# A 64-byte tile behind the parameter tile: everything allocated after it moves by 64 bytes

## What the kernel computes

```python
# block 1: a gated linear recurrence (stage A, OA), then forgetting attention (FG, F, OF)
x = x + (o * silu(gate)) @ a_w_out             # projections h @ w_in, 4 x 2048 columns
x = x + (attention(q, k, v, F) * silu(gate)) @ b_w_out
# block 2: recurrence and top-k attention side by side (X, C, OC)
x = x + (sigmoid(gr) * y_rnn + sigmoid(ga) * y_attn) @ w_o
# then a layer of 16384 experts, of which each token uses 8 x 16 (stages Q, U, V)
act = gelu(x . u[expert]) * gate               # 16 experts per head and token
x = x + sum(act * v[expert])
out = rmsnorm(x)
```

## The kernel before, in words

| tile | before | with the new tile |
|---|---|---|
| `xT`, `hh`, `hl` | 0 | 0 |
| `raw`, `wl`, `wh`, `iota`, `prm` | 64 | 64 |
| `ident`, `ones` (the pace), `ones_r`, `rstd`, `oT`, `sq`, `act`, `act_odd` | 64 | 0 |
| `kh`, `kl`, `uh_a`, `uh_c`, `ul_c`, `uh_q`, `ul_q`, `ckv_h`, `ckv_l` | 64 | 0 |
| `ah`, `al`, `gates_b`, `hot_a`, `kT_f`, `keysT`, `qp` | 64 | 0 |
| `uk_h`, `uk_l`, `uv_h`, `uv_l`, `xc`, `kT_c`, `qT_c`, `v_c`, `probT_c` | 0 | 64 |
| `AT`, `v_a`, `osq_a` | 32 | 96 |

## Time and profile before

### The profile page before, as it was taken

The page is one execution under the profiler, slowest core; times in us unless marked ns, Lnnn a source line. Parts: engine busy times, 40 slices in busy tenths (PEclk is TensorE's granted clock), DMA queues, the critical chain, the costliest instruction groups (busy, mean ns, idle before and its releaser), DMA issues.

```text
span 3275.2 us, 69109 instructions
## 1 busy us (share of the span) xinstructions
PE 3243.6 (99%) x28331; PEld 3211.1 (98%) x28331; DVE 2260.1 (69%) x3785; ACT 1685.3 (51%) x2279; POOL 33.8 (1%) x46
## 2 busy tenths in 40 slices
PE   9999999999999999999999999999999999999998
PEld 8999999999999999999999999999999999999998
DVE  8767667655566776666678987755676557788755
ACT  5444454767775556565554344444444444444444
POOL 4000000000000000000000000000000000000000
PEclk9999999999999999999999999999999999999999
DMA  5444445444445554545455555555555555555553
GB/s 189 153 148 166 144 162 182 155 155 165 159 162 183 194 171 164 189 164 188 167 188 174 187 181 181 182 185 184 181 180 182 183 186 184 180 175 173 180 182 140
DMA packets 98974, 569.29 MB, mean 174 GB/s; under 512 B 9440, under 2 KB 30304, under 8 KB 31584
## 3 DMA queue, kind: packets, MB, share of 16 engines
q1 hardware_dynamic: 98496, 565.49, 50.8%
q10 hardware_dynamic: 288, 1.05, 0.1%
HBM read 564.41 MB, written 2.10 MB: 173 GB/s over the span
## 4 chain that ended last, share of the span: by engine, by line
PE 90%; DVE 7%; DVEq 1%; ACT 1%; issue 1%; DMA 1%; POOL 0%; POOLq 0%; ACTq 0%; SPq 0%
PE bank L581 20%; PE bank L582 20%; PE bank L583 20%; PE bank L1069 8%; PE bank L1070 7%; PE bank L1071 7%; DVE wl L1652 2%; PE bank L1027 1%; PE bank L735 1%; PE bank L938 0%; PE bank L813 0%; PE bank L812 0%; PE bank L684 0%; DMA raw<-w_out_b 0%; PE bank L970 0%
## 5 line engine op out<-in xcount | busy, mean ns | idle before, releaser
L582 PE MATMUL bank<-hl,wh 128*128 128x256 f32 x5616 | 1563.5, 278 | 0.0
L1652 DVE TENSOR_TENSOR wl<-raw,wh 128x1024 fp32r<-128x1024 f32 x1052 | 1260.5, 1228 | 433.0 <-ACT wh L1151 425.7
L581 PE MATMUL bank<-hh,wh 128*128 128x256 f32 x5488 | 1546.3, 282 | 2.9 <-DVE wl L1652 2.5
L583 PE MATMUL bank<-hh,wl 128*128 128x256 f32 x5488 | 1525.8, 278 | 0.0
L1151 ACT ACTIVATE wh<-raw 128x1024 fp32r<-128x1024 f32 x1052 | 1051.3, 1049 | 270.4 <-DMA raw<-w_in_a 123.4
L582 PEld LDWEIGHTS bank<-hl,wh 128*128 128x128 f32 x5616 | 1060.1, 189 | 1.9 <-issue 1.7
L581 PEld LDWEIGHTS bank<-hh,wh 128*128 128x128 f32 x5488 | 1036.2, 189 | 7.3 <-issue 2.0
L583 PEld LDWEIGHTS bank<-hh,wl 128*128 128x128 f32 x5488 | 1033.7, 188 | 0.0
L1069 PE MATMUL bank<-ah,wh 128*128 128x256 f32 x2048 | 583.2, 285 | 1.4 <-DVE al L2360 1.4
L1071 PE MATMUL bank<-ah,wl 128*128 128x256 f32 x2048 | 580.2, 283 | 0.0
L1070 PE MATMUL bank<-al,wh 128*128 128x256 f32 x2048 | 580.2, 283 | 0.0
(11 more groups left out here) (412 smaller groups left out, 3178.2 us busy)
## 6 DMA issues: line engine op xcount, KB each, us to landing
raw<-peer_u SPq DMA_DIRECT2D x128, 1024.0 KB, 4.9
raw<-peer_v SPq DMA_DIRECT2D x128, 1024.0 KB, 4.8
raw<-w_in_c SPq DMA_DIRECT2D x64, 1024.0 KB, 4.9
raw<-w_in_a SPq DMA_DIRECT2D x63, 1024.0 KB, 4.8
raw<-w_kv SPq DMA_DIRECT2D x32, 1024.0 KB, 4.8
raw<-w_in_b SPq DMA_DIRECT2D x32, 1024.0 KB, 4.8
raw<-w_out_a SPq DMA_DIRECT2D x16, 1024.0 KB, 4.9
raw<-w_out_b SPq DMA_DIRECT2D x16, 1024.0 KB, 4.9
```

The lines of the kernel that those rows point to most:

```text
L581: eng.matmul(out, h_[:, k, :], high[:, k, :], start=(k == 0), stop=False)
L582: eng.matmul(out, h_[:, k, :], low[:, k, :], start=False, stop=False)
L583: last = eng.matmul(out, low_rows(c, k), high[:, k, :], start=False, stop=(k == KC - 1))
L1652: eng.tensor_tensor(low_half_out(c, half), raw_half(c, half), high_half(c, half).bitcast(F32), ALU.subtract).then_inc(lo_ready, 1)
```

## The change

A tile of 16 float32 per partition (64 bytes), which nothing reads or writes, is allocated behind `prm`. All tiles allocated after it start 64 bytes later. No instruction is added, removed or reordered.

```diff
         iota = sb("iota", [P, P])
         prm = sb("prm", [P, NPRM])
+        sb("prm_offset", [P, 16])
         fbias = sb("fbias", [FG_ROWS, 1])
         ident = sb("ident", [P, P])
         ones = sb("ones", [P, P])
```

## The result

| | before | after |
|---|---|---|
| median of 13 runs each, us | 3273.53 (3270.88 to 3277.77) | 3279.68 (3278.69 to 3287.05) |
| span of the profiled execution, us | 3275.2 | 3276.7 |

The ratio of the times is 1.0022, with a 95% interval of 1.0014 to 1.0031: the kernel became some 6 us slower, where 1.5% faster was forecast. All lines behind the new one have moved by one, so L582 of before is L583 here.

The account below looks back on a forecast made before the run. TensorE, busy for 99% of the span, was taken as the bound; 20.3 + 7.7 + 8.0 + 10.5 + 1.2 = 47.7 us less than the median 3273.5 gave 3225.8, forecast 3226 (own range 3215 to 3235, 8 in 10: 3215 to 3248).

Parts of the forecast that it names:

- VectorE's cover: In V2, VectorE's idle time was to leave it 0.70 us in a unit shortened to 5.80 us.
- The step that read the address: In TensorE's streams, a moving operand at 64 costs 3 to 7 ns more per 256-column matmul than one at 0.
- F and FG: Stages F and FG: 1584 matmuls with `kh`, `kl` go from 120.0 to 113.4 ns, 10.5 us less.
- V: Stages V0 to V3, matmuls with `ah`, `al`: 20.3 us less in V0 and V1, 7.7 in V2, 8.0 in V3.
- so I take the short gait: V0 and V1 follow a U stage without a break, so 113.4 ns a matmul: 20.3 us gained, against 7.1 otherwise.
- The openers: Float16 gate matmuls, which open units of U and V2: counted at 0, between 0 and 1 us by their small share.
- the pace loses its grip: Rival: moved `ones` and `gates_b` start `hh`, `hl` streams in the long gait; 61 us lost, net 47.5 slower, 3321; chance 0.05.
- The latent products: Stage C: `ckv` goes from 64 to 0 and `uv` from 0 to 64; 0.6 us gained and 0.6 lost.
- X: X's first units: 192 matmuls with `uh_c`, `ul_c` get 6.5 ns shorter each, 1.2 us less.
- Q: Q's first units: 0 of 1.2 us counted, since the routing on VectorE sets the pace and TensorE would wait longer.
- C and A: C's latent products cancel to 0; A's first pair counted at 0; A turning short, 6.9 us more, lay within the spread.
- no effect of the address: Rival: the operands, not their addresses, set the pitch in all streams; time 3273.5, within 0.2%; chance 0.04.

Follow-up runs that it names:

- E2: The kernel before with `ah` and `al` alone moved by 64 bytes per partition; 3243.06 us, ratio 0.9913.
- B1: The kernel before with `ah`, `al`, `kh`, `kl`, `uh_c`, `ul_c`, `uh_q`, `ul_q` all at distance 192 from the weights; 3236.60 us, ratio 0.9900.
- M1: A kernel of its own without the computation: streams of 72 matmuls over 64 address combinations, opened by column sum or pace; 113.3 to 120.0 ns a matmul.
- E1: The kernel before with the gate tiles (`hot_a`, `hot_b`, `gates_b`) moved by 64 and everything behind them by 128; 3294.18 us, ratio 1.0067.
- B2: B1 with two more pace matmuls a pair, one in stage A and one in C; 3227.71 us, ratio 0.9867 to before.
- E3: The kernel after with the gate tiles moved to 64 modulo 128 (192 modulo 256); 3264.72 us, ratio 0.9970 to before.
- E7: The kernel before with the pace's tile `ones` alone moved from 64 to 128 modulo 256; 3267.2 us against 3272.2, one run each.
- M2: A kernel of its own without the computation: 96 streams of 48 matmuls, each behind eight gate matmuls with tiles at varied places; 19 of 32 short at distance 192.

## Why the prediction was wrong, point by point

Two steps failed. The prediction made the moving tile's address the cause, where it is the distance of the two tiles; and it took the short gait for the new streams and counted the opening matmuls at nothing, where with the openers' tiles the gait changed. The kernel should have gained 47.7 us and lost 6.2.

**The bound was right.** Nothing but the pitch of TensorE's streams moved the time, the clock stood at 1.00 in the stretches shown, and no wait was added: in E2 and B1 the units of V2 took 5.80 us each, without one. VectorE's cover held.

**The step that read the address was wrong in its variable.** The prediction took "a moving operand at 64 costs more than one at 0" from the stretches. The rows were right. But `hh`, `ah` and `kh` all meet weights at one place, so with them the moving tile's address and its distance from the weights can't be told apart. Only the earlier trace rows could do that, and there the reading failed: `ckv` and `uv` were compared as if both had the main stream's weights beside them. Their stationary tiles are `uk` and `ckv`, at 0 and 192 modulo 256, and both distances are 192. Their two pitches were the two gaits of one distance. "Modulo 128" was the second half of the error: at distance 192 modulo 256 the short gait came in 15 of M1's 16 streams, at 64 in 2 of 16, and modulo 128 these two are the same.

**F and FG: 10.5 forecast, 4.9 measured,** of which 1.7 also lie between before and E2. `kh` went to distance 64, which is the long gait behind a pace in 8 of 8 streams of M1: 1584 x (120.0 - 117.8) = 3.5 us. B1 put it at distance 192 and gained 9.6 (7.9 against E2). The size of the term was nearly right for a change that was not made.

**V: 36.0 forecast, 9.8 measured.** Here the change did reach distance 192, and E2's profiled execution gives 35.5 for exactly these tiles (29.4 between the medians). The step that failed is "so I take the short gait": after has 117.8 in V0 to V3. In V2 each unit is opened by the gate tiles, so E1's mechanism explains it directly: 192.0 against E2's 185.8. V3 starts without a break at the pitch of V2, in after as in E2 and B1. For V0 and V1 the prediction's ground, that they follow a U stage "without a break between", was wrong: only their first six matmuls carry on the U stage's gait, and behind the longer step at the seventh the stream has a gait of its own. It was long in V0 and V1 of after and in V0 of B2, short in those of E2 and B1 and in V1 of B2. Whether a long gait ahead made the long one likelier in after is open.

**The openers: 0 to 1 us forecast, 18.6 us lost in U1 to U3.** After the 26.2 us missing in V this is the largest error, and the one that turned the sign: without it the kernel would have become some 12 us faster. In the sum the prediction priced the float16 gate matmuls by their own length and counted them at nothing, though it had noted that a stream's gait is set when it starts. An instruction that sets a state has to be priced by what runs in that state: 3 x 32 units x 0.20 us. E1 shows the loss with nothing else moved that TensorE reads in U, and in E3, with the gate tiles 64 further still, it is gone.

**The rival "the pace loses its grip"** had this mechanism, with a chance of 0.05, and was the nearest of all in kind. The gate tiles flipped their streams. Of the streams behind a pace only a few flipped, in C above all, and not by the place of `ones` (E7). So of the 14200 matmuls that this rival put at risk, 3 x 1536 of U1 to U3 flipped and few others, and its 61 us were 18.6, with the 2.7 of C beside them. (The 14200 are some 900 too many: OA's 600 and more of C were in the long gait in before too.)

**The latent products: 0 net forecast, 0 measured,** for another reason than the one given. **X: 1.2 forecast, 0.5 measured,** since `uh_c` went to distance 64 as `kh` did. **Q,** forecast at nothing: 0.1 us.

**C and A, forecast at 0:** +2.7 and -2.1, with OA -2.5. In C the eight streams behind the score products turned short in after (8 x 96 x 4.5 ns = 3.5 us less). The eight behind the latent products, eight behind a pace and four behind the value products turned long ((8 x 48 + 8 x 48 + 4 x 144) x 4.5 ns = 6.0 us more). The tiles that these openers read (`kT_c`, `uv_h`, `xc`, `probT_c`, `v_c`) all moved. E3 has the same, 452.6; E1, E2 and E7, in which these tiles stay, have 450.1 or 449.8. The -2.5 of OA are no effect of the change, as E1 and E2 show.

**The rival "no effect of the address"** (the prediction named the page "TensorE: Matmul & The Clock Gate" of the Trainium skill beside it) came out nearest in time, within 0.2%. That is luck: it is wrong in mechanism, and changes of 18.6 and 9.8 us happened to cancel. M1 shows seven different pitches for a form for which the section "Back-to-back issue gap" has one (262 cycles, 109.2 ns, as the gap of an isolated matmul), and none of them is as short.

## What to carry to other kernels

When two groups of rows differ in one property, list what else differs before that property is made the cause, and count the partner of an operand as part of it: here the pair's distance was the variable, and the one pair in the trace that could show it was misread. When a pitch has two values for the same instructions, find what opens the stretches and price every edit to the opener by the length of what follows it, not by its own. And a shift of all tiles is a change of many pairs at once: moving `ah` and `al` alone (E2) made the kernel 0.9% faster, moving everything 0.2% slower. Two profiles of kernels that are equal in a stage (E1 and E2 here) show how much of a difference there is chance.

## What the runs showed of the hardware that was not expected

- A stream of float32r matmuls of 256 columns, each with a weight load of its own, has a pitch that depends on the distance of its two tiles modulo 256: 113.3 at 192, 116.7 at 32, 117.3 or 118.6 at 160, 118.3 at 224, 118.7 or 119.9 at 128, 120.0 at 0 and 96, and 117.8, seldom 113.3, at 64 (M1). The clock was granted in full.
- At distance 192 there are two gaits, 113.3 and 117.8. A stream keeps its gait as long as its tiles stay the same and nothing breaks it: over 1400 matmuls in V0 of E2, over 1300 in that of after. At a break it can change: at V0's seventh matmul in B2, and when the latent products of C pass from `ckv` with `uk` to `uv` with `ckv`, at the same distance.
- The gait is set by what opens the stream. A pace of 64 float16 columns gave the short one in 8 of 8 streams of M1 and, put in by B2, in 15 of 15 behind column sums and score products. But 8 paced streams of C had the long one in after, so it is no sure means. Eight gate matmuls gave it in 19 of 32 (M2), and equal openings with equal addresses gave both. What draws it is open; the runs show that addresses take part in it and don't decide it alone.
- This draw also spreads the times of one kernel: B1's four runs lie between 3229 and 3244 us, and B2, whose A is paced, between 3226.7 and 3229.8. That the paces caused the smaller spread wasn't tested.
